# Weight buffers of a three-layer transformer kernel: three raw and four split panels outside layer 2

## What is computed

```
for i in (0, 1):
    h = rms_norm(x, norm_mix_pre[i]);  m = rms_norm(mem, norm_mem[i])
    mk, mv = split(m @ w_mem_kv[i])
    q, k, v, qm = split(h @ w_in[i])
    mixed = concat(attention_i(q, k, v), memory_attn(qm, mk, mv)) @ w_out[i]
    x = x + rms_norm(mixed, norm_mix_post[i])
    h = rms_norm(x, norm_ffn_pre[i])
    gate, up = split(h @ w_gu[i])
    x = x + rms_norm((silu(gate) * up) @ w_down[i], norm_ffn_post[i])

h = rms_norm(x, pre_mix_norm)                  # layer 2
xx = token_shift(h) - h
w, a, g from (h + xx * mu) @ (w1 | a1 | g1)    # the "lora" products
r, k, v, conv, z = h @ w_in                    # then WKV-7 and the convolution
x = x + rms_norm(merged @ w_out, post_mix_norm)
x = x + rms_norm(ffn(rms_norm(x, pre_ffn_norm)), post_ffn_norm)
```

## Time and profile before

| | before |
|---|---|
| median of 3 runs | 2431.65 us |
| lowest, highest | 2429.78, 2432.81 us |
| the profiled execution | 2432.14 us, of which the span of its instructions 2429.8 us |
| PE busy | 2329.2 us, 96% of the span |
| DVE, ACT, POOL busy | 1016.1, 877.9, 1004.8 us |
| mean granted TensorE clock | 0.978 of full |
| HBM read, written | 196.75, 12.41 MB |
| DMA queue of SP | 28.5% of 16 engines |

### The profile page before, as it was taken

One profiled execution on the slowest core, in us unless ns is written; L12 is line 12 of the kernel. 1 busy time (PEld: TensorE's weight loads), 2 busy tenths in 40 slices (PEclk: granted clock), 3 DMA queues, 4 the chain that ended last, 5 costly groups with the idle time before them and its releaser, 6 DMA issues.

```text
span 2429.8 us, 41306 instructions
## 1 busy us (share of the span) xinstructions
PE 2329.2 (96%) x17380; PEld 1913.5 (79%) x17380; DVE 1016.1 (42%) x1577; ACT 877.9 (36%) x1445; POOL 1004.8 (41%) x553
## 2 busy tenths in 40 slices
PE   7999999999899999999989999999999999999998
PEld 6867788888786778888867888686888777888886
DVE  6164522211465452221156987266343455322212
ACT  5174432222425442232243232635333244333222
POOL 4423544444542354444464444335000365444443
PEclk9999999999999999999999999989999899999999
DMA  6601333333431123333343333323000322333331
GB/s 172 150 17 53 98 102 96 94 95 98 106 99 36 37 77 96 97 100 91 98 118 91 97 100 107 100 74 114 4 4 4 140 71 80 93 98 101 91 96 66
DMA packets 386314, 210.30 MB, mean 87 GB/s; under 512 B 36928, under 2 KB 378664, under 8 KB 385876
## 3 DMA queue, kind: packets, MB, share of 16 engines
q1 hardware_dynamic: 383011, 196.78, 28.5%
q0 software_dynamic: 2448, 9.70, 1.0%
q10 hardware_dynamic: 672, 1.18, 0.1%
HBM read 196.75 MB, written 12.41 MB: 86 GB/s over the span
## 4 chain that ended last, share of the span: by engine, by line
PE 90%; DVE 3%; ACT 3%; issue 2%; POOL 2%; ACTq 0%; DMA 0%; POOLq 0%; DVEq 0%
PE ps L1958 24%; PE ps L1960 24%; PE ps L1959 24%; PE ps L2371 3%; PE ps L2358 2%; PE ps L2075 2%; PE ps L2336 2%; PE ps L2050 1%; PE ps L2060 1%; POOL x_res L750 1%; POOL w_lo L689 1%; PE ps L1917 1%; PE ps L2385 1%; PE ps L2038 1%; ACT w_hi L858 1%
## 5 line engine op out<-in xcount | busy, mean ns | idle before, releaser
L689 POOL TENSOR_TENSOR w_lo<-raw,w_hi 128x1024 fp32r<-128x1024 f32 (+2 forms) x344 | 811.2, 2359 | 947.7 <-ACT w_hi L858 943.9
L1958 PE MATMUL ps<-h_hi,w_hi 128*128 128x512 f32 x2016 | 802.3, 398 | 30.9 <-ACT h_hi L940 12.9
L1959 PE MATMUL ps<-h_hi,w_lo 128*128 128x512 f32 x2016 | 792.6, 393 | 0.0
L1960 PE MATMUL ps<-h_lo,w_hi 128*128 128x512 f32 x2016 | 792.3, 393 | 0.0
L858 ACT ACTIVATE w_hi<-raw 128x1024 fp32r<-128x1024 f32 (+2 forms) x344 | 356.9, 1038 | 1165.7 <-PE ps L1960 1160.6
L1958 PEld LDWEIGHTS ps<-h_hi,w_hi 128*128 128x128 f32 x2016 | 383.7, 190 | 126.4 <-issue 42.7
L1960 PEld LDWEIGHTS ps<-h_lo,w_hi 128*128 128x128 f32 x2016 | 383.3, 190 | 81.7
L1959 PEld LDWEIGHTS ps<-h_hi,w_lo 128*128 128x128 f32 x2016 | 384.1, 191 | 79.9 <-issue 1.6
L1958 PE MATMUL ps<-hid_hi,w_hi 128*128 128x512 f32 x528 | 205.4, 389 | 0.0
L1959 PE MATMUL ps<-hid_hi,w_lo 128*128 128x512 f32 x528 | 205.4, 389 | 0.0
L1960 PE MATMUL ps<-hid_lo,w_hi 128*128 128x512 f32 x528 | 205.4, 389 | 0.0
(11 more groups left out here) (328 smaller groups left out, 2654.1 us busy)
## 6 DMA issues: line engine op xcount, KB each, us to landing
raw<-in_w_gu SPq DMA_DIRECT2D x88, 512.0 KB, 3.8
raw<-in_w_in SPq DMA_DIRECT2D x56, 512.0 KB, 3.8
raw<-in_w_down SPq DMA_DIRECT2D x32, 448.0 KB, 3.7
raw<-in_ffn_w_gate SPq DMA_DIRECT2D x22, 512.0 KB, 3.8
raw<-in_ffn_w_up SPq DMA_DIRECT2D x22, 512.0 KB, 3.9
raw<-in_w_in_b SPq DMA_DIRECT2D x20, 512.0 KB, 4.4
raw<-in_w_down SPq DMA_DIRECT2D x16, 512.0 KB, 4.1
raw<-in_w_out SPq DMA_DIRECT2D x16, 512.0 KB, 4.0
```

The costliest lines, as they stand in the source:

```text
L689: nc.gpsimd.tensor_tensor(lo[:, k0:, :], src[:, k0:, :], hi[:, k0:, :].bitcast(f32), ALU.subtract).then_inc(lo_done, 1)
L1958: nc.tensor.matmul(bank, wh[:, k, :], ah[:, 0:width], start=first, stop=False)
L1959: nc.tensor.matmul(bank, wl[:, k, :], ah[:, 0:width], start=False, stop=False)
L1960: return nc.tensor.matmul(bank, wh[:, k, :], al[:, 0:width], start=False, stop=end)
```

## The change

- Outside layer 2's mixer (`wide`: panels below lora's first, and from out2's first on) there are three `raw` buffers (numbers 1 to 3, by `1 + p % 3`) and four split pairs (by `p % 4`). Inside it everything is as before.
- The two new split pairs lie in `spare` and in the memory of `raw` buffer 0: `w_lo3` is that buffer. So the first load into `raw` buffer 0 after down1, which is that of panel 192, waits until PE has used all panels of down1 (`sp.wait_ge(used, lora.p0)`).
- The attention outputs `o_raw` move into the last tiles of `h_hi` and `h_lo`. ACT's write of the last `h_hi` tile gets a wait for POOL's `h_lo` of the tile before.
- ACT and POOL split one panel further ahead: `groups` by `more`, the norms by `ahead_of_norm` (3, but 2 for down1).
- The splitting in halves stays for lora and rwkv_out only.

```diff
+        for i in range(2):
+            w_hi.append(at(f"w_hi{2 + i}", [P, KD, P], spare + 8192 * i, f32r))
+            w_lo.append(at(f"w_lo{2 + i}", [P, KD, P], spare + 8192 * i + 4096, f32r))
...
-        o_raw = at("o_raw", [P, 2, TOK], spare + 2048)
+        o_raw = [at(f"o_raw{i}", [P, TOK], h_off + 16384 * i + 7 * 2048) for i in range(2)]
...
+        HALF_SPLIT = ("lora", "rwkv_out")
...
+        def wide(p):
+
+            return p < lora.p0 or p >= L["out2"].p0
+
+        raw_slot = [1 + p % 3 if wide(p) else p % 4 for p in range(len(panels))]
+        split_slot = [p % 4 if wide(p) else p % 2 for p in range(len(panels))]
...
+        def ahead_of_norm(name):
+
+            return 2 if name == "down1" else 3
...
-                if p >= 4:
-                    sp.wait_ge(lo_done, p - 3)
+                if raw_before[p] is not None:
+                    sp.wait_ge(lo_done, raw_before[p] + 1)
+                if raw_slot[p] == 0 and wide(p - 4):
+                    sp.wait_ge(used, lora.p0)
...
-                    if p >= 2:
-                        pool.wait_ge(used, p - 1)
+                    if split_before[p] is not None:
+                        pool.wait_ge(used, split_before[p] + 1)
...
-                split_lo(L[name].p1 + 2)
+                split_lo(L[name].p1 + ahead_of_norm(name))
...
-                    split_hi(last + 1)
+                    more = 1 if wide(last + 2) and wide(l.p0) else 0
+                    split_hi(last + 1 + more)
                     act.wait_ge(used, last)
                     if not (name in BEFORE_NORM and i == l.groups - 1):
-                        split_hi(last + 2)
+                        split_hi(last + 2 + more)
...
-                    if c == 6 and name in PAIRED:
-                        split_hi_half(name)
...
-                split_hi(L[name].p1 + 2)
+                split_hi(L[name].p1 + ahead_of_norm(name))
...
                 def output(tile):
                     act.wait_ge(sg["o_norm"], 8 * layer + tile + 1)
+                    if tile == 7:
+                        act.wait_ge(hl, KD * v0 + 7)
```

More of the change, by code:

```diff
@@ L423, in build, with before @@
         block = ctx.enter_context(nc.Block())
+        lora = L["lora"]
+        PAIRED = ("gu0", "q1", "gu1", "lora", "rwkv_out", "gu2")
+        HALF_SPLIT = ("lora", "rwkv_out")
+        in_halves = {L[name].p0 + 2: i + 1 for i, name in enumerate(HALF_SPLIT)}
+        def wide(p):
+            return p < lora.p0 or p >= L["out2"].p0
+        raw_slot = [1 + p % 3 if wide(p) else p % 4 for p in range(len(panels))]
+        split_slot = [p % 4 if wide(p) else p % 2 for p in range(len(panels))]
+        def before(slots, p):
+            same = [q for q in range(p) if slots[q] == slots[p]]
+            return same[-1] if same else None
+        raw_before = [before(raw_slot, p) for p in range(len(panels))]
+        split_before = [before(split_slot, p) for p in range(len(panels))]
         loaded_at, count = [], [0] * 4
         for p, pan in enumerate(panels):
[L429 to L433, removed]
+            count[raw_slot[p]] += 80 if pan.by_side else 32 if pan.split else 16
+            loaded_at.append(count[raw_slot[p]])
         def freed(eng, g):
@@ L696, in scale_raw @@
                 if k0 == 0:
-                    pool.wait_ge(loaded[p % 4], loaded_at[p])
+                    pool.wait_ge(loaded[raw_slot[p]], loaded_at[p])
                 for k in range(k0, k1):
                     for half in range(2):
-                        r = raw[:, p % 4, k, 64 * half:64 * half + 64]
+                        r = raw[:, raw_slot[p], k, 64 * half:64 * half + 64]
                         last = nc.gpsimd.tensor_scalar(r, r, vec("mu_wag_2", k, half), None, ALU.mult)
@@ L725, in output @@
                     pool.wait_ge(hh, KD * (3 if layer == 0 else 6) + tile + 1)
-                    nc.gpsimd.tensor_tensor(h_lo[:, tile, :], o_raw[:, k, :], h_hi[:, tile, :].bitcast(f32), ALU.subtract
+                    nc.gpsimd.tensor_tensor(h_lo[:, tile, :], o_raw[k][:, :], h_hi[:, tile, :].bitcast(f32), ALU.subtract
                                             ).then_inc(hl, 1)
@@ L759, in _ @@
             add_residual("down0", h_out)
[L760 removed]
+            split_lo(L["qm1"].p1 + 3)
             attention(1)
@@ L850, in split_hi @@
                         act.wait_ge(sg["raw_scaled_g"], 1)
-                    act.wait_ge(loaded[p % 4], loaded_at[p])
-                    if p >= 2:
-                        act.wait_ge(used, p - 1)
+                    act.wait_ge(loaded[raw_slot[p]], loaded_at[p])
+                    if split_before[p] is not None:
+                        act.wait_ge(used, split_before[p] + 1)
                     k0 = 0
```

38 lines of the change are left out of this document (19 added, 19 removed).

## The result

| | before | after |
|---|---|---|
| median of the runs taken together | 2430.72 us (4 runs) | 2450.84 us (4 runs) |
| profiled execution | 2432.14 us | 2449.99 us |
| its span | 2429.8 us | 2448.2 us |
| ratio of the times, 95% interval | | 1.0076 [1.0064, 1.0089] |

The change makes the kernel 0.76% slower by the ratio, some 18.5 us (15.6 to 21.6); the medians are 20.1 us apart, the spans 18.4. The forecast was 0.55%, 2445.0 us; the median is 0.8 us above the range.

The account below looks back on a forecast made before the run. PE, busy 96% of the span, was taken as the bound. Lora seam 13.1, start 0.5, halves -0.2 sum to 13.4 us on the profiled 2432.14, 2445.5; median forecast 2445.0 us, range 2440.0 to 2450.0.

Parts of the forecast that it names:

- The hold and the queue: Down1 to lora: 192 waits for PE, 193 to 195 queue behind; 194 lands 8.3 us after PE's end.
- rival (a): Down1 to lora: the loads do not overlap at all, delay 18.3 us, 2450.2 us; chance 11%.
- POOL's chain: Down1 to lora: two splits and two scalings, 11.43 us from 194's landing, delay POOL's additions by 13.1 us.
- The delay of the additions is the delay of the pair: Lora's pair: it ends as much later as POOL's additions start later, 13.1 us.
- the chunks, not PE, ended last before, and will again: Lora's pair: the chunks set its end, so their 13.1 us delay counts, not PE's 11.1 us.
- a slow start by itself costs nothing: Start of lora: up to 2 us of slower start at PE's clock is free, since chunks set the pace.
- nothing behind the pair gives it back: Behind lora's first pair: third and fourth panel go on from the pair's end as before, recovering nothing.
- rwkv_out to out2: 0: Before out2: panel 268 waits for the split of 266 but lands with 2 us to spare; cost 0.
- Both waits at the start: Kernel start: PE's waits of 1.25 and 1.92 us for w_lo stay despite the fourth split pair.
- the copies of mv: Kernel start: the first values' copies wait behind panel 6's rounding, +0.5 us, between 0 and 1.5.
- The rival (d): Faster: buffers end the start's waits for weights and the hold is covered, 2428.1 us; chance 3%.
- The steady stretches: Steady stretches: seven panels held ahead instead of six change nothing, 0 either way.

Follow-up runs that it names:

- Experiment 2: Kernel before, only the hold added: SP waits ahead of loading panel 192 until PE has used 191; 2447.64 us, 1.0057 of before.
- 1: Changed kernel, lora's panels kept in three raw buffers and the hold moved from panel 192 to 196; 2434.47 us, 1.0005 of before.
- 5: Changed kernel, SP loads panels 193, 194 and 195 first and the held 192 last; 2442.12 us, 1.0044 of before.
- Experiment 6: Changed kernel, at down1's end POOL's addition of chunk c waits for DVE's x_lo of chunk c-2; 2449.36 us, 1.0080 of before.
- 3: Changed kernel, ACT doesn't round panel 270 ahead at out2's first group; 2448.50 us, 1.0063 of before.
- 4: Changed kernel, hold moved to panel 196 and no rounding ahead at out2's first group; 2432.95 us, again 2434.11 us, both 1.0001 of before.
- 8: Kernel of experiment 4, ACT's rounding of panels 1 to 3 moved earlier, panel 6 back behind the values' copies; 2426.40 us (0.9986), again 2427.48 (0.9984).

## Why the prediction was right, and where it was wrong

**The hold and the queue: right.** SP issued 192 0.4 us behind the start of PE's last matmul. POOL's wait for 194 ended at 1242.56, 8.7 us after the first issue (forecast 8.3 from PE's end on), by which rival (a), loads that don't overlap at all and take 13.5, falls. The root came at 1241.81 (forecast 1241.3). Experiment 2 shows the hold to be the cause, 1 that without it nothing is left, 5 that the loads and POOL's work behind it, and not only the held panel, set the time.

**POOL's chain: right, a little short.** 11.43 us was forecast, and it took 12.2 (1242.56 to 1254.78): the ten scalings took 5.16 us, not 4.16. From down1's last matmul (1233.76 before, 1233.47 after) to the first addition it was 7.0 us and is 21.3, so the additions are 14.3 us late where 13.1 was forecast; that is 1.2 us of the miss.

**"The delay of the additions is the delay of the pair": mis-sized.** 13.1 was forecast and 16.0 measured for the seam. 14.3 of it is the additions' delay. The rest, 1.7 us, arose inside the pair, where I had let the pace of the chunks be as before and up to 2 us of a slower start be free. 0.5 us of it is the chunks': from the first addition to the end of the last `x_lo` it is 14.3 us in after and was 13.8. The other 1.2 us is PE's: before, its last matmul began 1.4 us behind the end of the last `x_lo`, and in after 2.6 us. What failed is the step "the chunks, not PE, ended last before, and will again". DVE's second `x_lo` stood still for three of POOL's additions, PE waited 2.36 us for it, and PE was then behind the chunks to the end of the pair. Before, the first `x_lo` (1241.92) came just ahead of POOL's second addition (1241.99), and from there on the two engines took turns, `x_lo` taking 1.10 to 1.47 us. Experiment 6 takes PE's lag away, loses a part of that at the additions, and gets back 0.8 us.

That a slow start by itself costs nothing is borne out as far as the traces go: in experiments 5 and 6 the clock was low for the first 5 us of the pair, and PE kept up with the chunks. In after it was low for 9 us, with the wait in between; no run separates the wait from the clock there. Against "nothing behind the pair gives it back": conv_in took 1.4 us less in after than in before. But it took 0.4 us less in experiment 2 and 0.3 in experiment 1, which has no such seam, so that is not shown to be the change's doing.

**"rwkv_out to out2: 0": wrong.** I had looked only at whether panel 268 had landed (it had, with 0.6 us to spare, not 2), not at the split of 270, which now stood beside DVE's last `m_lo`. It cost 3.6 us in after, and experiments 1, 3 and 4 show it come and go with that one panel: in the four traces that have the panel ahead (after, 1, 5, 6) the stretch takes 2.1 to 3.6 us more than in before, and in those of 3, 4 and 8 at most 0.1 more. 2.0 us of it, the wait, is the same in all four; the rest is the lower clock behind it, which lasted for different times. The prices are the traces': the ratios differ by 3.2 us between after and 3 and by 1.0 between 1 and 4, each with some 4 to 5 us to either side. 13.4 + 2.9 (seam) + 3.6 make 19.9 us. The medians differ by 20.1 us; by the ratio it is 18.5, by the spans of the two profiled executions 18.4, of which conv_in's 1.4 us would fill the gap. So these two steps hold the miss.

**The rest: right.** Both waits at the start stayed (0.8 and 1.9 us), and the copies of mv moved behind panel 6 for 0.5 us; the upper bound of 1.5, for a load that lands in 5.3 us, was passed in two other executions (2.0 and 2.2). The rival (d), that the buffers end these waits, falls by after itself, and experiment 8 shows why: it wants the rounding elsewhere in ACT's queue. The steady stretches were worth 0 (experiment 4). The attention's new wait cost nothing that shows. The halves at q1 brought 0.4 us, where 0.2 had been taken.

## What to carry to other kernels

A buffer carved out of other memory brings a hold with it, and in an in-order DMA queue every load behind the held one inherits it: put the hold where the next panels are not urgent, which here took two lines. Ahead of an operation moved or added on POOL, look at what DVE does beside it, also where POOL itself has time to spare. And a wait for weights is not always a lack of buffers: read first where the step that makes them stands in its engine's queue.

## What the hardware showed that I had not expected

In these traces a DVE operation with both tensors in SBUF is not slowed in proportion beside POOL's: it stands still until POOL's operation is done, and ends 0.55 us after it. The four additions in after end at 1254.78 + 4.96 = 1259.74, the `x_lo` begun inside the second ends at 1256.84 + 3.45 = 1260.29. The two splits at out2 end at 2009.45 + 5.23 = 2014.68, the `m_lo` at 2009.57 + 5.66 = 2015.23. In experiment 6 the additions end at 1258.32 and the `x_lo` at 1258.87. DVE's `h_out`, which reads one tensor from PSUM, took 0.73 to 0.75 us everywhere at the seam, beside POOL or not. The other side pays too: an addition beside running DVE work took 1.72 us at 1261.03 (5.12 for three), and the four in a row began 1.24 apart.

The Trainium skill (SBUF — State Buffer, Who interferes with whom) says this of the two engines: a DVE instruction with two SBUF inputs contends with a GpSimd one that reads SBUF, what they share is held as an exclusive lock, and the order of issue decides who blocks. The traces agree in all three places. Who gets the next turn when both have work ready is less plain. In after the `x_lo` waited not only for the addition that was running (which ended at 1257.3) but for the two behind it, 2.7 us more than its own 0.74, where one addition is 1.24. But that was seen once. At out2 DVE got its turn between two splits in a row (2.89 and 2.84 us, one split for each `m_lo`), and in before and in experiment 5, where POOL made seven additions without a break, each `x_lo` waited for no more than the one that was running (at most 1.47 us). What made the difference in after, no run here shows.
